# Delta rule on raw keys, with the inverse applied in each scan step and weight slabs computed between the steps

## The reference

```python
q, k = _l2_norm(q), _l2_norm(k)            # divided by sqrt(sum of squares + 1e-6)
# per direction, head and chunk; g: cumulated log decay, beta: gate
decay = exp(where(incl, g[..., :, None] - g[..., None, :], -inf))
a_mat = where(strict, einsum(kb, k) * decay, 0)           # kb = k * beta
sol   = triangular_solve(eye + a_mat, [v * beta, kb * exp(g)])   # u, w
# scan over the chunks
v_new = u_i - w_i @ state
o_i   = q_i @ state + qk_i @ v_new
state = state * exp(gl_i) + k_i.T @ v_new
# after both directions
o = _rms_norm(o_f + flip(o_b), dn_gain) * silu(z_dn)
```

## Time and profile before

| what | value |
|---|---|
| time, median of 3 runs | 3041.14 us (3039.02 to 3042.1) |
| profiled execution, span from first to last instruction | 3042.0 us (no time of its own is listed for it) |
| TensorE busy | 2950.7 us, 97% |
| VectorE busy | 2110.4 us, 69% |
| ScalarE busy | 1411.3 us, 46% |
| GpSimd busy | 488.3 us, 16% |
| mean granted TensorE clock | 0.991 of full speed |

### The profile page before, as it was taken

One profiled execution on the slowest core, in us unless ns is written; L12 is line 12 of the kernel. 1 busy time (PEld: TensorE's weight loads), 2 busy tenths in 40 slices (PEclk: granted clock), 3 DMA queues, 4 the chain that ended last, 5 costly groups with the idle time before them and its releaser, 6 DMA issues.

```text
span 3042.0 us, 51632 instructions
## 1 busy us (share of the span) xinstructions
PE 2950.7 (97%) x18980; PEld 2547.3 (84%) x18980; DVE 2110.4 (69%) x3097; ACT 1411.3 (46%) x2279; POOL 488.3 (16%) x392
## 2 busy tenths in 40 slices
PE   7999999999999999999999999999999999999998
PEld 4888888887789988777789988799988777799886
DVE  5566665446489954888789944799646986899635
ACT  3655565444356622334456622566423334566422
POOL 0213123157420011000200012100110000300012
PEclk9999999999999999999999999999999999999999
DMA  6121120213322322222323232232222222233322
GB/s 254 44 61 43 28 69 16 68 63 105 110 83 98 104 97 89 94 87 83 104 90 106 97 104 97 87 108 99 99 95 92 89 84 83 97 111 102 106 94 79
DMA packets 97248, 275.15 MB, mean 90 GB/s; under 512 B 35712, under 2 KB 36864, under 8 KB 95760
## 3 DMA queue, kind: packets, MB, share of 16 engines
q1 hardware_dynamic: 94016, 267.89, 26.5%
q10 hardware_dynamic: 2768, 4.25, 0.4%
q0 software_dynamic: 320, 1.05, 0.1%
HBM read 267.88 MB, written 5.28 MB: 90 GB/s over the span
## 4 chain that ended last, share of the span: by engine, by line
PE 87%; DVE 6%; ACT 4%; issue 2%; DMA 1%; SPq 0%; ACTq 0%; DVEq 0%
PE bank L149 16%; PE bank L151 16%; PE bank L150 16%; PE bank L2024 8%; PE bank L2025 8%; PE bank L2026 8%; PE bank L1598 1%; ACT weights_hi L137 1%; PE bank L1612 1%; PE bank L1664 1%; PE bank L2515 1%; DVE weights_lo L142 1%; PE bank L1667 1%; PE bank L1677 1%; DMA mod_weights<-w_mod 1%
## 5 line engine op out<-in xcount | busy, mean ns | idle before, releaser
L142 DVE TENSOR_TENSOR weights_lo<-weights_raw,weights_hi 128x1024 fp32r<-128x1024 f32 (+2 forms) x258 | 395.5, 1533 | 326.3 <-ACT weights_hi L137 323.0
L137 ACT ACTIVATE weights_hi<-weights_raw 128x1024 fp32r<-128x1024 f32 (+2 forms) x250 | 285.1, 1140 | 460.2 <-PE bank L151 447.8
L149 PE MATMUL bank<-x_hi,weights_hi 128*128 128x512 f32 x832 | 337.0, 405 | 5.1 <-DVE x_lo L1914 3.0
L151 PE MATMUL bank<-x_hi,weights_lo 128*128 128x512 f32 x832 | 326.4, 392 | 0.0
L150 PE MATMUL bank<-x_lo,weights_hi 128*128 128x512 f32 x832 | 325.3, 391 | 0.0
L2024 PE MATMUL bank<-sum_hi,block_hi 128*128 128x256 f32 x960 | 271.1, 282 | 4.6 <-ACT bank L2176 3.6
L150 PE MATMUL bank<-hidden_lo,weights_hi 128*128 128x512 f32 x704 | 273.9, 389 | 0.0
L149 PE MATMUL bank<-hidden_hi,weights_hi 128*128 128x512 f32 x704 | 273.9, 389 | 0.0
L151 PE MATMUL bank<-hidden_hi,weights_lo 128*128 128x512 f32 x704 | 273.9, 389 | 0.0
L2025 PE MATMUL bank<-sum_lo,block_hi 128*128 128x256 f32 x960 | 270.6, 282 | 0.0
L2026 PE MATMUL bank<-sum_hi,block_lo 128*128 128x256 f32 x960 | 269.4, 281 | 0.0
(11 more groups left out here) (451 smaller groups left out, 7466.4 us busy)
## 6 DMA issues: line engine op xcount, KB each, us to landing
raw_pair<-w_ff1in SPq DMA_DIRECT2D x42, 1024.0 KB, 4.9
raw_pair<-w_ff2in SPq DMA_DIRECT2D x42, 1024.0 KB, 4.9
weights_raw<-w_mix SPq DMA_DIRECT2D x72, 512.0 KB, 3.2
weights_raw<-w_ff1out SPq DMA_DIRECT2D x32, 704.0 KB, 4.0
weights_raw<-w_ff2out SPq DMA_DIRECT2D x32, 704.0 KB, 4.0
weights_raw<-w_tail SPq DMA_DIRECT2D x42, 512.0 KB, 3.3
mod_weights<-w_mod SPq DMA_DIRECT2D x6, 2048.0 KB, 16.4
weights_raw<-w_dn SPq DMA_DIRECT2D x24, 512.0 KB, 3.4
```

The lines of the kernel that those rows point to most:

```text
L137: nc.scalar.activation(K.wh[:, slot, 0:cols], K.raw[:, slot, 0:cols], ACT.Copy).then_inc(S.wh_ready, 1)
L142: nc.vector.tensor_tensor(K.wl[:, slot, 0:cols], K.raw[:, slot, 0:cols], K.wh[:, slot, 0:cols].bitcast(F32), ALU.subtract).then_inc(S.raw_ ...
L149: nc.tensor.matmul(out, K.wh[:, slot, a:b], xh, start=start, stop=False)
L151: return nc.tensor.matmul(out, K.wl[:, slot, a:b], xh, start=False, stop=stop)
```

## The change

- Keys and queries stay raw. `turn_heads` turns keys, queries and values once, by tile; the `products` are of raw keys and queries as they come out of the convolution. The inverse of the keys' squared length (`K.n2`) is multiplied into system and scores, the key's length into the values (`K.knorm`, on GpSimd), and the inverse square into the tail decays (`K.tail2`). The query's length is not applied: its floor goes into the last norm (`K.fq`). `unit`, `turn_back`, `turn_queries`, their copies and the roots for each tile are gone.
- The preparation is one loop over the tiles: heads, exponents and products of tile t + 1 after one part of fill (two in group 0). The heads are turned in bank 3, the exponents made in bank 4 alone. ScalarE does `squares(t + 1)` before `decays(t)`.
- `solved` and `keep` are gone. Each scan step has `against` (raw keys by state), VectorE's `residual`, `renew` (inverse by residual), ScalarE's copy, `grow`, VectorE's new state. The step 0 has `renew` and `grow` in the level steps 14 to 17.
- Outputs are made by token: `answer` (queries by state) in bank 5, scaled by ScalarE, and `inner` (scores by new values) in bank 7, joined by VectorE, or for two of the steps by VectorE and GpSimd.
- `take(later, ...)` runs one part in each of the level steps 13 to 17 and three in each scan step: 20 parts of the next set in groups 0 and 1, 16 in groups 2 and 3; for group 3 these are the first two slabs of the tail (`AHEAD`).
- In the tail the norm is by token: VectorE sums along the row, ScalarE scales the head, TensorE turns it (four transposes), VectorE multiplies once.
- Taps are taken earlier: 4 after the tiles, 6 after the small inverses, one in each of the first six level steps and two in the others.

```diff
         def squares(t):
             n = TILES * G + t
             w = 4 if t < 4 else 2
             act.wait_ge(S.tk_ready, n + 1)
-            act.wait_ge(S.hss_ready, n)
-            nc.scalar.activation(K.junk[:, 0:w, :], pb[3 + t % 2][:, 0:128 * w].rearrange("p (c v) -> p c v", v=128), ACT.Square)\
+            if n > 0:
+                act.wait_ge(S.hss_ready, n)
+            nc.scalar.activation(K.junk[:, 0:w, :], pb[3][:, 0:128 * w].rearrange("p (c v) -> p c v", v=128), ACT.Square)\
                 .then_inc(S.hsq_ready, 1)
+            nc.scalar.activation(K.ks[:, t, 0:2, :], pb[3][:, 0:256].rearrange("p (c v) -> p c v", v=128), ACT.Copy)\
+                .then_inc(S.kt_ready, 1)
             act.wait_ge(S.tv_ready, n + 1)
-            nc.scalar.activation(K.vs[:, t, :, :], pb[5][:, 0:256].rearrange("p (j v) -> p j v", v=128), ACT.Copy)\
...
             act.wait_ge(S.gate_step, GATE_STEPS)
-        act.wait_ge(S.ks_ready, TILES * G + TILES + CREDIT)
-        act.wait_ge(S.qs_ready, 4 * G + 4)
         for t in range(TILES):
-            if t < 4:
-                queries_back(t)
+            if t + 1 < TILES:
+                squares(t + 1)
             decays(t)
-            if t == 3 and not more:
-                act_gate(act, 1)
+            if t == 3 and more:
...
+        def norms(t):
             n = TILES * G + t
             w = 4 if t < 4 else 2
             dve.wait_ge(S.hsq_ready, n + 1)
             nc.vector.tensor_reduce(K.ssq[:, t, 0:w], K.junk[:, 0:w, :], AX.X, ALU.add).then_inc(S.hss_ready, 1)
...
+            if t == 4:
                 split_lo(dve, s + 1, 1, 1024)
+        nc.vector.tensor_tensor(K.tail2[:, :, :].rearrange("p t (d j) -> p t d j", j=2),
...
+        def residual(n, tiles):
+
+            for d, t in enumerate(tiles):
+                dve.wait_ge(S.sk_ready, 10 * G + 2 * n + d - 1)
+                if n == 1:
+                    dve.wait_ge(S.vm_ready, G + 1)
+                for j in range(2):
+                    c, at = 2 * d + j, 8 * d + 2 * G + j
+                    ins = nc.vector.scalar_tensor_tensor(out=K.rr[:, c, :], in0=pb[scan_bank(n, d)][:, 128 * j:128 * j + 128],
+                                                         scalar=K.negeg[:, t, at:at + 1], in1=K.vs[:, t, j, :],
+                                                         op0=ALU.mult, op1=ALU.add)
+                ins.then_inc(S.r_ready, 1)
+
...
+    def tail_begin(pe):
+        return chain(*[slab_parts(pe, TAIL_SLAB + i, TAIL_EVIC + i, i % 2, False) for i in AHEAD])
+
     def pe_group(pe, G, fills):
         s, v = DN_SLAB + 6 * (G + 1), DN_EVIC + 6 * (G + 1)
-        fill = fills[G]
-        later = fills[G + 1] if G + 1 < GROUPS else iter(())
+        fill, later = fills[G], islice(fills[G + 1], 20 if G + 2 < GROUPS else 16)
...
+        def turn_heads(t):
+
             n = TILES * G + t
-            w = 4 if t < 4 else 2
-            pe.wait_ge(S.kqn_ready, n - 1 + CREDIT)
             lo = 128 * t
-            for c in range(w):
-                src = K.hv[HEAD_SLABS.index(((1, 0), (1, 1), (0, 0), (0, 1))[c])]
-                last = nc.tensor.transpose(pb[3 + t % 2][:, 128 * c:128 * c + 128], src[:, lo:lo + 128], K.ident[:, :])
+            if t > 0:
+                pe.wait_ge(S.kt_ready, n)
+            for c in range(4 if t < 4 else 2):
+                src = keys(G, c) if c < 2 else queries(G, c - 2)
+                last = nc.tensor.transpose(pb[3][:, 128 * c:128 * c + 128], src[:, lo:lo + 128], K.ident[:, :])
             last.then_inc(S.tk_ready, 1)
-            pe.wait_ge(S.vs_ready, n + CREDIT)
+            if t > 0:
+                pe.wait_ge(S.vs_ready, n)
             for j in range(2):
-                last = nc.tensor.transpose(pb[5][:, 128 * j:128 * j + 128], K.hv[HEAD_SLABS.index((2, j))][:, lo:lo + 128], K.ident[:, :])
+                last = nc.tensor.transpose(pb[7][:, 128 * j:128 * j + 128], K.hv[HEAD_SLABS.index((2, j))][:, lo:lo + 128], K.ident[:, :])
...
             if t > 0:
-                turn_back(t - 1)
-        take(fill, (3, 1, 1, 0)[G])
-        turn_back(TILES - 1)
-        pe.wait_ge(S.kq_ready, TILES * G + TILES + CREDIT)
-        pe.wait_ge(S.vs_ready, TILES * G + TILES + CREDIT)
-        if G == 0:
-            pe.wait_ge(S.rows_kept, MOD_BLOCKS + 3)
-
...
-                turn_queries(t)
-            rows(t)
-            products(t)
-            take(fill, 1)
+            take(fill, 1 if G else 2)
+            if t + 1 < TILES:
+                turn_heads(t + 1)
+                rows(t + 1)
+                products(t + 1)
         take(fill, 99)
-        pe.wait_ge(S.qd_ready, 4 * G + 4 + CREDIT)
...
+        def renew(n, d, t):
+
+            if n:
+                pe.wait_ge(S.r_ready, 10 * G + 2 * n + d - 1)
+            else:
                 pe.wait_ge(S.evac, v + (6 if G + 1 < GROUPS else 8) + CREDIT)
-            pe.wait_ge(S.e_ready, STEPS_LEVEL * G + STEPS_INNER + k + 1 + CREDIT)
-            pe.wait_ge(S.ek_ready, n + 1)
-            if n > 0:
-                pe.wait_ge(S.uw_kept, 2 * n)
-            for c in range(4):
-                last = nc.tensor.matmul(pb[0][:, part(c)], K.ek[k % 2][:, c, :], K.e[:, c, t, :], start=True, stop=True)
+                pe.wait_ge(S.vm_ready, G + 1)
+                pe.wait_ge(S.e_ready, STEPS_LEVEL * G + STEPS_INNER + d + 1 + CREDIT)
...
         for i in range(STEPS_LEVEL):
             product(i)
             if i > 0:
                 correction(i - 1)
             if i + 3 < STEPS_LEVEL:
                 turn_inverse(i + 3)
-            if i >= STEPS_INNER + 2:
-                solved(i - STEPS_INNER - 2)
+            if i in (STEPS_INNER + 2, STEPS_INNER + 3):
+                renew(0, i - STEPS_INNER - 2, TILE_ORDER[i - STEPS_INNER - 2])
+            if i in (STEPS_INNER + 4, STEPS_INNER + 5):
+                if i == STEPS_INNER + 4:
+                    pe.wait_ge(S.ks_ready, 2 * (G + 1))
+                grow(0, i - STEPS_INNER - 4, TILE_ORDER[i - STEPS_INNER - 4])
+            if i > STEPS_INNER:
+                take(later, 1)
         correction(STEPS_LEVEL - 1)
-        pe.wait_ge(S.ks_ready, TILES * G + TILES + CREDIT)
-        pe.wait_ge(S.uw_kept, 2 * (TILES * G + 2))
-        pe.wait_ge(S.e_ready, STEPS_LEVEL * (G + 1) + CREDIT)
-        grow(0, TILE_ORDER[0:2])
-        solved(4)
-        against(1, (5, 4))
-        grow(1, (5, 4))
-        solved(5)
-        pe.wait_ge(S.qkd_ready, 4 * G + 4)
         for n, (f, b, x) in enumerate(scan_steps()):
-            if x is None:
+            if n == 0:
                 continue
-            if x < 2:
-                pe.wait_ge(S.uw_kept, 2 * (TILES * G + 2 * x + 4))
-            against(n, (f, b))
-            if x == 3:
-                take(later, 2)
-            if x > 0:
-                pe.wait_ge(S.ot_ready, 8 * G + 2 * x)
-            for c, t in enumerate((f, f, b, b)):
-                nc.tensor.matmul(pb[7][:, part(c)], K.st[1 - n % 2][:, c, :], K.qd[:, t, c, :], start=(c == 0), stop=False)
+            tiles = (f, b)
+            for d, t in enumerate(tiles):
+                against(n, d, t)
+            if x is not None:
+                answer(n, x, tiles)
+            take(later, 1)
+            if n == 1:
+                pe.wait_ge(S.e_ready, STEPS_LEVEL * (G + 1) + CREDIT)
+            for d, t in enumerate(tiles):
+                renew(n, d, t)
+            take(later, 2)
             if n < 5:
-                grow(n, (f, b))
-            else:
-                for d in range(2):
-                    pe.wait_ge(S.vn_ready, 2 * (5 * G + n) + d - 1)
-            for c, t in enumerate((f, f, b, b)):
-                last = nc.tensor.matmul(pb[7][:, part(c)], K.vn[:, c, :], K.qkd[:, t, c, :], start=False, stop=(c == 3))
-            last.then_inc(S.so_ready, 1)
-        take(later, 2)
+                for d, t in enumerate(tiles):
+                    grow(n, d, t)
+            if x is not None:
+                if x == 0:
+                    pe.wait_ge(S.qkd_ready, 4 * G + 4)
+                inner(n, x, tiles)
+        pe.wait_ge(S.oa_ready, 4 * G + 4)
         pe.wait_ge(S.ot_ready, 8 * G + 8)
 
...
+                if i not in AHEAD:
+                    pe_slab(pe, a, b, slot, False)
             else:
...
                 n = NORMED[i]
-                pe.wait_ge(S.nrstd_ready, n + 3)
+                pe.wait_ge(S.hsc_ready, n + 1)
                 if n > 0:
-                    pe.wait_ge(S.on_ready, n)
+                    pe.wait_ge(S.zs_used, gates_until(n - 1))
                 for t in range(4):
-                    last = nc.tensor.matmul(pb[5][:, 128 * t:128 * t + 128], K.hstd[:, 4 * n + t:4 * n + t + 1].to_broadcast([128, 128]),
-                                            K.ident[:, :], start=True, stop=True)
+                    last = nc.tensor.transpose(pb[5][:, 128 * t:128 * t + 128], K.ot[:, n, t, :], K.ident[:, :])
                 last.then_inc(S.head_wide, 1)
 
...
```

(5 more changed lines are left out.)

## The result

The changed kernel takes 3104.9 us (median of 4 runs, 3102.9 to 3109.4) against 3041.5 us: a ratio of 1.021, 95% interval 1.020 to 1.023. It is 63 us slower; I had said 30. The profiled executions differ by 59 us (spans of 3101.3 and 3042.0 us), so the rows can carry nearly all of the account.

The account below looks back on a forecast made before the run. TensorE, busy for 97% of the span, was taken as the bound, with the chain to the first inverse turn as a second one. Groups +27, tail -10 and clock +13 gave 3041 + 30 = 3071 us; range 3038 to 3097.

Parts of the forecast that it names:

- the serial loop: Preparation: TensorE and ScalarE take turns, `rows(t+1)` waiting for `decays(t)`; period 5.4 us, TensorE idle 2.2 to 2.3 of it.
- the first turns: First inverse turn, ending each group's preparation: 65.5, 61.7, 61.7 and 66 us after the first transpose, without the clock term.
- The scan: Five scan passes with an extra round trip: 32.8 us in groups 0 and 1, 30.5 in groups 2 and 3.
- I take a third, +13.: Lower TensorE clock after pauses, mainly in the preparations: a third of the upper bound of 41 us, +13 us.
- my upper bound: Clock term: 1.5 us lost at each preparation pause, plus stretches after waits at inversion, state and tail; 41 us in all.
- rival (b): TensorE's clock falls at nearly every pause, costing 30 to 41 us; total 3088 to 3099 us, chance 0.17.
- fill at 4.1 us instead of 2.3.: Preparation's first round: the first fill part waits for slab 2's split, behind tile 0's squares and norms; 4.1 us, formerly 2.3.
- The chain decides: Preparation's end: the chain from last system matrix to first inverse turn gives 61.7 us; TensorE's own work ends at 60 to 61.5.
- 2.4 us for the state: Inversion's end: TensorE's first `against` waits for state copies behind VectorE's update and taps; 2.4 us, 1.2 in group 3.
- 1.5 for ScalarE's head pairs: Inversion: ScalarE's head and centre pairs move to steps 2, 8 and 12; 1.5 us added, plus 1.0 at step 12.
- about 7 us idle: Tail start: TensorE waits for GpSimd, ScalarE and VectorE, about 7 us; of 20.8 us less TensorE work, 10 gained.
- 49 us less work for TensorE: Whole kernel: removed transposes, halved `solved` products and lighter tail work take 49 us off TensorE.

Follow-up runs that it names:

- experiment 2: Changed kernel with idle products of 128 columns of ones where TensorE waits in the preparation, order unchanged; 3070.9 us, ratio 1.010.
- experiment 4: Changed kernel with VectorE's first-state copies ahead of the inversion's last update and the last two convolution taps behind the first residual; 3091.5 us, ratio 1.017.
- experiment 5: On top of experiment 1, GpSimd clears a group's inverse tiles only after tile 0's exponentials, not at the first transpose; 3036.0 us, ratio 0.998.
- experiment 7: Changed kernel with the changes of experiment 1, experiment 4 and experiment 5, plus ScalarE's head activations and centre taps in separate level steps; 3010.4 us, ratio 0.990.
- 9: experiment 7 with GpSimd's additions over the rows of the pooling window left out for heads 0 to 5; 3010.9 us, ratio 0.990.
- 10: As 9, with slabs 10 and 11 split before the tail's wait for GpSimd, in free banks, and head 0 turned in slab 11; 3009.6 us, ratio 0.989.
- experiment 1: Changed kernel with ScalarE taking tile t's exponentials before the squares and copies of tile t + 1; 3043.1 us, ratio 1.001.

## Why the prediction was wrong

Right were the direction, the serial loop (place, waiter, releaser; 1.6 to 2.1 us at tiles 2 to 5 against the 2.2 to 2.3 forecast), and the first turns once the clock is out of it (experiment 2). The scan came near (127.2 us against 126.6), but by luck: the terms that I listed add up to 32.0 and 29.0 us a group, not to 32.8 and 30.5. At a clock of 1.00 that is what they are (31.9, 31.9, 29.9 and 28.9 in experiment 4); in the changed kernel the low clock behind the wait for the state filled the difference. The numbers fail at these steps:

- **The clock: "I take a third, +13."** This is the step that failed: the term was 13, and it measured 34. Filling the pauses gave 34 us back, 32 of it in the preparations. That is 8.1 us a group, more than the 7.5 that my upper bound had for the pauses: a fall came at most of them, and the first round of group 1 ran for 13.7 us on end at a clock of 0.54. My rows for it, the two windows of the earlier trace rows, were single pauses between dense stretches, and I scaled them down instead of asking what a stretch made of little else than pauses does. My rival (b) had the mechanism and up to 3099, still 6 us short. The Trainium skill (TensorE: Matmul & The Clock Gate, "A second HAM failure mode: psum-queue depth-cycling") says that frequent small pauses make the clock swing; here the trace agrees for pauses of 1.6 to 2.1 us in each round, by 34 us, while rests of 0.5 to 1.1 us in the same rounds left the clock at 1.00.
- **Preparation, first round: "fill at 4.1 us instead of 2.3."** It came at 5.6. I had the contention with GpSimd only under the taps; it sat on a tiny addition ahead of the split (2.07 us), and with the clear out of the way the part comes at 4.1 (experiment 5). The longest stretch of low clock begins behind this wait.
- **"The chain decides"** when the first inverse turn comes: no. In the changed kernel TensorE's own work runs right up to it (the idle products start at 336.73 us and last 1.95, the turn comes at 338.51 us in group 1, and TensorE has no wait there in any group); with its slow rounds it was the later one. The forecast was hardly touched by this, since it had both at 60 to 62.
- **Inversion: 2.4 us for the state and 1.5 for ScalarE's head pairs**: the wait was 3.2 us, and 1.6 more of low clock in the scan behind it (experiment 4). The pairs cost 1.87 and 0.9 us of waits, and more with what they brought on: experiment 7 took 2.8 to 4.2 us off the inversions of groups 0 to 2. For group 3 the listed terms give 34.7 us, not the 33.9 that I wrote; it took 34.9. Together 11 us over.
- **Tail: "about 7 us idle", and only 10 of the 20.8 us gained.** It was 8.15 idle and 6 gained; right in kind, 4 us short. Of the reasons that I gave, GpSimd is a small one: a quarter of its work less gives some 2 us (9, 10). That VectorE holds the rest is not shown.
- **49 us less work for TensorE** was right: in experiment 7, with the clock at 1.00 in the four groups, TensorE is busy for 2898.1 us, 52.6 less than before, and the kernel comes out 31 us faster.

## What to carry to other kernels

When a buffer is shared from turn to turn, look at the order on the engine that empties it: what the other engine waits for goes first, and that was worth 62 us here for a swap of two calls. Price a pause of TensorE twice, as idle time and as slower work behind it; the loop here, with a 2 us pause in each round, paid more for the second (34 us) than for the first (28). To find out which is which, fill the pause with idle products.

## What I had not expected of the hardware

- 0.5 to 1.1 us of pause in each round left the granted clock at 1.00 (experiment 2), while 1.6 to 2.1 us in each round, with 2.8 and 3.3 us in the first one, brought 0.83 over the whole preparation of group 1.
- Equal pauses did not always bring the same. The pair of 0.60 and 0.47 us that comes with a clock of 0.74 in group 2 of the kernel before stands in its group 1 too, and the window around it there (261 to 268 us) has 1.00. In experiment 1 the wait of 3.2 us before the first `against` came with a scan of 33.5 us at 0.95 in group 0 and of 31.9 us at 1.00 in group 1. So the length of one pause doesn't settle whether the clock falls.
- A `tensor_scalar` on 128x4 elements lasted 2.07 and 1.60 us instead of 0.17, each time to the end of a GpSimd memset; in all groups of all runs of the changed kernel the two ends lie within 0.03 us; a reduction of 128x512 elements beside it kept its time (0.69 us).
